# Attention on one core: GpSimd joins the differential maps in two operations, VectorE takes second turned copies, ScalarE's first copies go between exponentials

## The reference

```
A  4 heads  softmax(q k^T + window and distance bias) v     (dilated windows)
B  8 heads  softmax(q k^T) v                                (latent attention, rotary part)
C  4 heads  a = softmax(q_u k_u^T - slope * distance), u = 0, 1
            o = (a[0] - lam * a[1]) v                       (differential heads)
```

## Time and profile before

| what | value |
|---|---|
| median of 3 runs | 3202.36 us |
| profiled execution | 3200.54 us, its span 3198.7 us |
| granted TensorE clock, mean | 0.999 |
| attention stretch, layer 0 | 1476 to 1608 us of the span |
| attention stretch, layer 1 | 2598 to 2730 us |
| PE, DVE, ACT, POOL busy over the span | 99%, 58%, 17%, 8% |

### The profile page before, as it was taken

How to read it: one execution, slowest core, us unless ns; L and a number is a source line. 1 busy time by engine, 2 the same in 40 slices (tenths; PEclk the granted TensorE clock), 3 DMA queues, 4 the chain that set the end, 5 groups by cost and what they waited for, 6 DMA issues and landing times.

```text
span 3198.7 us, 36062 instructions
## 1 busy us (share of the span) xinstructions
PE 3165.5 (99%) x14174; PEld 2575.5 (81%) x14174; DVE 1867.6 (58%) x3244; ACT 532.1 (17%) x1120; POOL 240.8 (8%) x218
## 2 busy tenths in 40 slices
PE   9999999999999999999999999999999999999999
PEld 3888758888888888885488888888888854788887
DVE  6356845764347764465676664466644656766643
ACT  2111122000111000115621000110001157210001
POOL 1244410000000000003000000000000030000000
PEclk9999999999999999999999999999999999999999
DMA  5254321222222222223012222222222230122221
GB/s 239 81 183 147 143 79 53 93 79 93 85 90 82 90 89 86 89 74 119 7 66 79 93 84 91 90 79 93 86 89 89 74 119 7 61 85 93 79 84 61
DMA packets 43881, 288.28 MB, mean 90 GB/s; under 512 B 5405, under 2 KB 5405, under 8 KB 12737
## 3 DMA queue, kind: packets, MB, share of 16 engines
q1 hardware_dynamic: 39024, 271.14, 23.9%
q0 software_dynamic: 4688, 14.85, 1.4%
HBM read 281.76 MB, written 2.11 MB: 89 GB/s over the span
## 4 chain that ended last, share of the span: by engine, by line
PE 93%; DVE 4%; ACT 1%; DVEq 1%; issue 1%; DMA 0%; POOL 0%; ACTq 0%
PE ps L872 77%; PE ps L574 3%; PE ps L1283 2%; PE ps L1316 2%; PE ps L1009 2%; PE ps L1228 1%; PE ps L1297 1%; DVE arena L1953 1%; PE ps L555 1%; PE ps L899 1%; PE ps L1255 0%; PE ps L1248 0%; ACT arena L1640 0%; PE ps L956 0%; PE ps L969 0%
## 5 line engine op out<-in xcount | busy, mean ns | idle before, releaser
L872 PE MATMUL ps<-arena 128*128 128x256 f32 x5456 | 1244.9, 379 | 0.1
L872 PEld LDWEIGHTS ps<-arena 128*128 128x128 f32 x5456 | 1037.5, 190 | 140.6 <-DVE arena L2126 0.5
L872 PE MATMUL ps<-arena,ring 128*128 128x256 f32 x2768 | 646.0, 379 | 0.5 <-ACT arena L1368 0.5
L872 PEld LDWEIGHTS ps<-arena,ring 128*128 128x128 f32 x2768 | 526.0, 190 | 71.6 <-ACT arena L1368 0.9
L872 PE MATMUL ps<-xn,ring 128*128 128x256 f32 x2272 | 518.9, 379 | 5.6 <-DVE arena L1769 2.1
L872 PEld LDWEIGHTS ps<-xn,ring 128*128 128x128 f32 x2272 | 431.5, 190 | 71.4 <-issue 9.3
L1763 DVE TENSOR_TENSOR arena<-arena,ps 128x512 f32<-128x512 f32 x173 | 118.9, 687 | 545.1 <-PE ps L872 487.8
L1736 DVE TENSOR_TENSOR arena<-ring 128x512 f32<-128x512 f32 (+1 forms) x194 | 131.1, 676 | 347.9 <-PE ps L872 347.8
L872 PE MATMUL ps<-xn,arena 128*128 128x256 f32 x1264 | 302.2, 379 | 0.0
L872 PEld LDWEIGHTS ps<-xn,arena 128*128 128x128 f32 x1264 | 240.4, 190 | 32.4
L1556 ACT ACTIVATE arena<-arena 128x512 f32<-128x512 f32 x88 | 55.4, 630 | 883.6 <-DVE arena L2245 883.6
(11 more groups left out here) (327 smaller groups left out, 2510.2 us busy)
## 6 DMA issues: line engine op xcount, KB each, us to landing
ring<-in_w_up_a SPq DMA_DIRECT2D x44, 1024.0 KB, 4.8
ring<-in_w_up_b SPq DMA_DIRECT2D x44, 1024.0 KB, 4.8
ring<-in_w_ff SPq DMA_DIRECT2D x32, 1024.0 KB, 4.8
ring<-in_w_ada SPq DMA_DIRECT2D x24, 1024.0 KB, 4.9
ring<-in_w_down_a SPq DMA_DIRECT2D x16, 1024.0 KB, 4.8
ring<-in_w_down_b SPq DMA_DIRECT2D x16, 1024.0 KB, 4.8
ring<-in_w_in SPq DMA_DIRECT2D x14, 1024.0 KB, 4.8
ring<-in_w_out SPq DMA_DIRECT2D x12, 1024.0 KB, 5.6
```

What stands on the lines that cost most here:

```text
L872: mm = nc.tensor.matmul(out_ap, w, operand(product, quads[i]), start=at not in opened, stop=last_chunk and i == len(quads) - 1, skip_group ...
```

## The change

Four edits, all within the attention loop:

1. `copied_by` loses its exception: ACT makes every first copy and DVE every second copy of A and B steps. These are 12 copies a layer (steps 1 to 3, 9 to 11, 17 to 19, 25 to 27).
2. DVE's `join` becomes `factor`: the two one-column operations remain, the 128x512 operation goes.
3. POOL gets `join`: after the factor it multiplies the second map by it (tensor_scalar) and adds the result to the first (tensor_tensor), 16 times a layer. `window(6)` moves ahead of `bias(4)`, the joins of C0 stand before `bias(4)`, those of C1 before `window(7)`, the rest behind `bias(7)`.
4. ACT's loop runs the first exponential of step n, the first copy of step n-3, the second exponential, and then the second copy where it is ACT's (odd C steps have theirs on DVE).

```diff
 def copied_by(n, u):
-    if u and step(n)[0] != "C" and n + 3 < ATT_STEPS and step(n + 3)[0] == "C":
-        return "act"
     return ("act", "dve")[u]
...
+            def join(layer, n):
+                _, g, i = step(n)
+                pool.wait_ge(sem("factors"), 16 * layer + joins(n) + 1)
+                first, second = prob(2 * n), prob(2 * n + 1)
+                nc.gpsimd.tensor_scalar(second, second, other[:, g % 2, 2, i:i + 1], None, ALU.mult)
+                pool.drain()
+                nc.gpsimd.tensor_tensor(first, first, second, ALU.add).then_inc(sem("joined"), 1)
...
                 window(layer, 5)
+                window(layer, 6)
+                for n in C_STEPS[:ST]:
+                    join(layer, n)
                 bias(layer, 4)
-                window(layer, 6)
                 bias(layer, 5)
                 bias(layer, 6)
+                for n in C_STEPS[ST:2 * ST]:
+                    join(layer, n)
                 window(layer, 7)
                 bias(layer, 7)
+                for n in C_STEPS[2 * ST:]:
+                    join(layer, n)
...
                 for n in range(ATT_STEPS + 8):
                     if n < ATT_STEPS:
-                        exps(n)
+                        exp(n, 0)
+                    if 0 <= n - 3 < ATT_STEPS:
+                        turned(n - 3, 0)
+                    if n < ATT_STEPS:
+                        exp(n, 1)
                     for t in VALUES_AT.get(n, ()):
                         take_values(t)
                     if 0 <= n - 3 < ATT_STEPS:
-                        turned(n - 3)
+                        turned(n - 3, 1)
...
-                    nc.vector.scalar_tensor_tensor(by, one, col("neg_lam"), inv, ALU.mult, ALU.mult)
-                    dve.drain()
-                    first, second = prob(2 * n), prob(2 * n + 1)
-                    nc.vector.scalar_tensor_tensor(first, second, by, first, ALU.mult, ALU.add).then_inc(sem("joined"), 1)
+                    nc.vector.scalar_tensor_tensor(by, one, col("neg_lam"), inv, ALU.mult, ALU.mult)\
+                        .then_inc(sem("factors"), 1)
```

More of the change, by code:

```diff
@@ L238 @@
 WINDOW_AT = [0, 1, 2, 3, 0, 1, 2, 0]
+C_STEPS = [n for n in range(ATT_STEPS) if step(n)[0] == "C"]
 A_STEPS = [n for n in range(ATT_STEPS) if step(n)[0] == "A"]
@@ L1627, in take_values, with exp @@
                     nc.scalar.activation(v_b[:, t, :], bank_ap("uv", t), ACT.Copy).then_inc(evacuated("uv", t), 1)
-                def exps(n):
+                def exp(n, u):
                     kind, g, i = step(n)
                     place = set_of(n)
[L1632 to L1642, removed]
@@ L1644, in turned @@
-                def turned(n):
-                    kind, g, i = step(n)
[L1646 to L1652, removed]
+                    unit = 2 * n + u
@@ new lines, in exp @@
+                    act.wait_ge(sem("minima"), UNITS_2 * layer + unit + 1)
+                    dst = prob(unit)
+                    if kind == "C":
+                        total = sums_p[:, place, g % 2, i:i + 1] if u == 0 else other[:, g % 2, 0, i:i + 1]
+                    else:
+                        total = sums_p[:, place, u, i:i + 1]
+                    nc.scalar.activation(dst, ps[:, 2 * (n % 2) + u, :] if kind == "B" else dst, ACT.Exp,
+                                         bias=minima[:, unit % 8:unit % 8 + 1], scale=1.0 if kind == "B" else -1.0,
+                                         accum_out=total).then_inc(sem("exps"), 1)
@@ new lines, in turned @@
+                def turned(n, u):
+                    kind, g, i = step(n)
+                    if kind == "C" and u != i % 2 or copied_by(n, u) != "act":
+                        return
+                    wait_turned(act, (layer, "turn", n, u))
+                    dst = probs_t[2 * set_of(n) + (g % 2 if kind == "C" else u)][:, :, i * P:(i + 1) * P]
+                    nc.scalar.activation(dst, turn_bank((layer, "turn", n, u)).rearrange("p (t s) -> p t s", t=ST),
+                                         ACT.Copy).then_inc(sem("turns_act"), 1)
@@ L2379, in least, with factor @@
                         last.then_inc(sem("minima"), 1)
-                def join(n):
+                def factor(n):
                     _, g, i = step(n)
@@ L2435, in _ @@
                     if 0 <= n - 1 < ATT_STEPS and step(n - 1)[0] == "C":
-                        join(n - 1)
+                        factor(n - 1)
                     if pair_ending(n - 1) is not None:
```

## The result

The changed kernel needs 3209.26 us (median of 13 runs, 3206.29 to 3211.68), the kernel before 3201.82 us in 13 runs beside it: ratio 1.0020, 95% interval 1.0013 to 1.0027. The forecast was 3197.5 us with a range up to 3206. The profiled execution took 3209.72 us (its span is 3208.0), 9.2 us more than the profiled one before; by the medians it is 7.4 us more.

The account below looks back on a forecast made before the run. PE bounds the kernel, busy 99%; only its 13.5 us of attention waits can be won. Per layer 3.9 + 0.67 - 1.2 - 0.93 = 2.4 us, 4.9 in two: 3202.36 - 4.9 = 3197.5 us, range 3190.5 to 3206.

Parts of the forecast that it names:

- POOL's join: Attention loop, join on POOL: tensor_scalar 0.80, gap 0.16, tensor_tensor 1.28, together 2.24 us, and 0.30 to wake.
- the slower rival: Attention loop: POOL can't keep pace, decided from a tensor_scalar of about 1.5 us; 3211 us, chance 0.14.
- The 0.16 between the operations: POOL's join in attention: POOL leaves 0.16 us between the dependent tensor_scalar and tensor_tensor.
- end of the stretch: End of each attention stretch: PE's 1.63 us wait for an ACT copy behind one exponential too many; 0.67 us won a layer.
- (a): B steps 9, 25 and 33: a first copy between the exponentials makes scores 0.4 us late; 1.2 us lost a layer.
- (b): C1's joins delay the last window's bias, `least(19)`, and step 17's second turn; 0.93 us lost a layer.
- The waits on ACT's copies: PE in attention: the 0.32, 0.26 and 1.63 us waits for copies late in ACT's loop would go.
- The groups' win: Four C groups in attention: the weigh starts 0.97 us earlier in each, 3.9 us won a layer.
- rival F: Attention: more is won if the small factor operation doesn't wait, 1.4 us a group (C2 1.2); 3193.7 us, chance 0.38.
- S: POOL can't keep pace: with the tensor_scalar at 2.07 a join takes 3.5 us; 9 us lost, 3211 us, chance 0.14.
- The shared read path: SBUF reads of DVE and POOL: `factor(13)` would wait until POOL's join ends, 0.4 us on DVE.

Follow-up runs that it names:

- sem_join: Changed kernel with a semaphore in place of POOL's drain between the join's tensor_scalar and tensor_tensor; ratio 0.9996 against the kernel before.
- early_window: Changed kernel with the last window's DMA issued ahead of the fourth join of C1 instead of behind it; ratio 1.0010 against the kernel before.
- warm: Changed kernel with a tiny tensor_scalar and tensor_tensor pair, with drains, on POOL ahead of each layer's first join; ratio 1.0002 against the kernel before.
- best: Changed kernel with broadcast tensor_tensor multiplication, semaphore for the drain, and last window ahead of C1's fourth join; 3191.09 us, ratio 0.9964 against the kernel before.
- tt_sem: Changed kernel with the join's multiplication as a broadcast tensor_tensor and a semaphore for the drain; 3193.91 us, ratio 0.9972 against the kernel before.

## Why the prediction was wrong

**The step that failed is "POOL's join", "A join is then 0.80 + 0.16 + 1.28 = 2.24 us".** The tensor_scalar costs 1.56, which lies inside the bounds (0.52 to 2.07) but beyond the point of 1.5 from which the slower rival was to decide and the prediction called itself wrong. A join takes 2.98 us where the sum had 2.24. I scaled the affine select's 0.29 for 128 columns; an operation of another kind was a weak row for the value. The GPSIMD Engine Reference of the Trainium skill, section 3.1, has a tight loop of 1.8 cycles an element, from which the 0.77 us came, and about 2.6 cycles for tensor_tensor; it gives no figure for tensor_scalar. Read as one for tensor_scalar, as the prediction did, it has the order of the two wrong: the trace has tensor_scalar at 1.56 and tensor_tensor at 1.27, so the measurement decides.

The 0.16 between the operations failed in one place of each layer: 2.13 us in the first join, from the drain, as sem_join shows; that it waits there because of POOL's window DMAs is what early_window and warm suggest. The row for it came from the sums of the first block, not from behind window DMAs.

**No term for the clock.** Every term took PE at full speed. That held in the attention stretches of the profile of before, whose longest wait there was 1.63 us. The waits of 2.69 and 1.87 us brought two falls a layer in this execution, 1.7 us each.

Of one layer, won (+) and lost (-) against before, from PE's scores rows set side by side:

| term | forecast | measured |
|---|---|---|
| C0 | +0.97 | -2.9 (gap, late join, one fall) |
| C1, C2, C3 | +0.97 each | +0.72 each |
| end of the stretch | +0.67 | +0.66 |
| (a) B steps | -1.2 | -1.26 |
| (b) last window | -0.93 | -3.76 (wait and one fall) |
| sum | +2.4 | -5.1 |

What the runs show of the same 5 us, each step the difference of two traced stretches, from `best` at 127.4 us upwards: the late window 0.7 (tt_sem 128.1), the tensor_scalar 3.1 (sem_join's layer without a fall, 131.2), the drain 2.2 (changed without falls, 133.4), two falls 3.4 (136.8). The tensor_scalar's price is a third of these 9.4 us. PE's waits of layer 0 account for it: in sem_join four waits of 0.64 us for the first joins of the groups and 1.71 at step 17, in tt_sem 0.50 at step 17 and one of 0.36 for VectorE. Yet either cause alone, taken away, brings the kernel level with before (0.9992 and 0.9996): one fall is left in attention in each of their traces, where the changed kernel has four. With the multiplication at 1.04 us, above my 0.80, the time comes out near the forecast's ratio of 0.9985, the gap still there.

**What was right.** The waits on ACT's copies went, the end was won to 0.01 us, (a) cost what was said, and (b) went by the chain described, only four times as long. The groups' win was even undersized: `best` is 4.4 us a layer ahead, and with the end's 0.66 and (a)'s 1.26 that is 1.25 for each of four groups, near rival F's 1.4.

**The rivals.** S was right on the side and near on the time (3211 against 3209.3), but not in its sum: its late fourth join (1.8 us) brought no wait, and the falls and the gap stood in its place. The shared read path was real: `factor` stretched to 1.13 us, till the end of POOL's tensor_tensor, and SBUF — State Buffer of the Trainium skill, Who interferes with whom, agrees with that row. But it followed from POOL's slowness and did not bring the loss. In sem_join it is blocked more and the loss is gone; in `best`, whose joins also read both maps, its median is 0.22 and the longest 0.53. No wait of PE above 0.1 us in the changed kernel's attention ends on VectorE, and the blocked factor delays POOL little: behind it POOL starts its next join 0.12 us after the one before (1528.86, behind 1527.46 + 1.28), without it at once (1498.22).

## What to carry to other kernels

An engine's price for an operation that the trace does not show needs the nearest kind of operation, and where the bounds straddle the point that decides, the chance of the bad side should be large. When a dependent pair on GpSimd stands behind DMAs which that engine issues, look for a gap between the two, and try a semaphore in place of the drain. When TensorE runs back to back, count behind each new wait as long as those here a possible fall of the clock, here worth 1.7 us.

## What the runs showed of the hardware

- GpSimd, 128x512 float32: tensor_scalar 1.56 us with a column factor and 1.49 with a constant, tensor_tensor 1.27 (an addition), and 1.04 for a multiplication with one operand broadcast from a column.
- The gap that a drain on GpSimd left between two operations was 3.76 us with a DMA issued just ahead of the pair (warm), 1.56 with one just ahead (early_window), 2.13 with the last one 9 us ahead (C0), and only 0.25 with the last one 16 us ahead (C2 of the changed kernel); otherwise 0.15. A semaphore in its place left 0.08. So a DMA issued since the last drain does not suffice for a long gap. What the drain waits for was not settled.
- In attention the clock falls, of about 1.7 us each, stood behind waits of TensorE from 1.25 to 2.8 us, and other waits of that length brought none. Near the end of the program the clock of the kernel before falls too, at 3190.7 us, behind waits of only 0.25 and 0.57 us, so the length of a single wait does not decide. The changed kernel's runs spread over 5 us, those of `best` over 2.3.
